# A decoder layer's first two gate/up units: half of the second unit is moved in among the first

## What is computed

```python
mod = jax.nn.silu(c) @ w_ada[l] + b_ada[l]
sh1, sc1, g1, sh2, sc2, g2, sh3, sc3, g3 = jnp.split(mod, 9, axis=-1)
h = modulate(rms_norm(x, norm_ffn1[l]), sh1, sc1)        # h * (1 + scale) + shift
x = x + 0.5 * g1[:, None, :] * swiglu(h, w1_gate[l], w1_up[l], w1_down[l])
```

## Time and profile before

| | before |
|---|---|
| median of three runs | 2169.45 us |
| the profiled execution, its time / its span | 2164.42 / 2162.6 us |
| TensorE matmul, weight load | 96%, 76% busy |
| VectorE, ScalarE, GpSimd | 62%, 42%, 2% busy |
| moved by DMA | 513.21 MB, mean 237 GB/s |
| mean granted TensorE clock | 0.976 |

### The profile page before, as it was taken

One profiled execution on the slowest core, in us unless ns is written; L12 is line 12 of the kernel. 1 busy time (PEld: TensorE's weight loads), 2 busy tenths in 40 slices (PEclk: granted clock), 3 DMA queues, 4 the chain that ended last, 5 costly groups with the idle time before them and its releaser, 6 DMA issues.

```text
span 2162.6 us, 28599 instructions
## 1 busy us (share of the span) xinstructions
PE 2077.0 (96%) x9500; PEld 1633.5 (76%) x9500; DVE 1337.4 (62%) x1774; ACT 904.7 (42%) x1139; POOL 42.8 (2%) x63
## 2 busy tenths in 40 slices
PE   6899999999999999899979899899999999999997
PEld 2468888888877778788847877788888888877776
DVE  1447767677778887866645765577664444444444
ACT  3334444434443333444334544444444444433332
POOL 0100000000000000000004000000000000000000
PEclk7999999999999999999979999999999999999999
DMA  9968787788788888678686405478775666646553
GB/s 363 386 230 288 269 298 272 262 278 286 270 285 311 299 299 303 226 260 287 222 266 226 139 21 179 137 242 275 267 255 182 186 184 184 184 156 222 185 185 127
DMA packets 271077, 513.21 MB, mean 237 GB/s; under 512 B 15193, under 2 KB 29572, under 8 KB 270504
## 3 DMA queue, kind: packets, MB, share of 16 engines
q1 hardware_dynamic: 270120, 508.37, 70.2%
q10 hardware_dynamic: 896, 4.06, 0.5%
HBM read 508.50 MB, written 3.87 MB: 237 GB/s over the span
## 4 chain that ended last, share of the span: by engine, by line
PE 90%; DMA 4%; DVE 3%; issue 1%; ACT 1%; POOL 0%; SPq 0%; DVEq 0%; ACTq 0%; POOLq 0%
PE ps L623 28%; PE ps L624 28%; PE ps L625 28%; DMA ada_half<-in_w_ada_dram 3%; DMA ada_raw<-in_w_cmp_k_dram 1%; PE ps L665 1%; PE ps L707 1%; PE ps L652 1%; PE ps L777 1%; PE ps L681 1%; DMA ada_raw<-in_w_cmp_v_dram 0%; PE ps L733 0%; DVE ada_acc L1450 0%; PE ps L879 0%; PE ps L1039 0%
## 5 line engine op out<-in xcount | busy, mean ns | idle before, releaser
L1432 DVE TENSOR_TENSOR w_lo<-raw,w_hi 128x1024 fp32r<-128x1024 f32 (+1 forms) x657 | 792.5, 1219 | 407.3 <-ACT w_hi L1129 403.3
L1129 ACT ACTIVATE w_hi<-raw 128x1024 fp32r<-128x1024 f32 (+1 forms) x657 | 686.5, 1054 | 815.2 <-PE ps L625 583.9
L623 PE MATMUL ps<-w_hi,hT_hi 128*128 128x512 f32 (+1 forms) x1856 | 741.8, 400 | 8.1 <-POOL hT_lo L584 2.6
L624 PE MATMUL ps<-w_lo,hT_hi 128*128 128x512 f32 (+1 forms) x1856 | 734.2, 396 | 0.0
L625 PE MATMUL ps<-w_hi,hT_lo 128*128 128x512 f32 (+1 forms) x1856 | 733.9, 395 | 0.0
L623 PEld LDWEIGHTS ps<-w_hi,hT_hi 128*128 128x128 f32 x1856 | 351.5, 189 | 96.3 <-issue 7.2
L625 PEld LDWEIGHTS ps<-w_hi,hT_lo 128*128 128x128 f32 x1856 | 351.2, 189 | 84.2
L624 PEld LDWEIGHTS ps<-w_lo,hT_hi 128*128 128x128 f32 x1856 | 351.7, 189 | 82.1 <-issue 1.0
L1450 DVE SCALAR_TENSOR_TENSOR ada_acc<-ada_raw,silu_c,ada_acc 128x512 f32<-128x512 f32 x420 | 315.3, 751 | 7.9
L623 PE MATMUL ps<-w_hi,actT_hi 128*128 128x512 f32 x704 | 283.7, 403 | 3.4 <-DVE silu_gate L1563 3.4
L625 PE MATMUL ps<-w_hi,actT_lo 128*128 128x512 f32 x704 | 279.1, 396 | 0.0
(11 more groups left out here) (202 smaller groups left out, 977.7 us busy)
## 6 DMA issues: line engine op xcount, KB each, us to landing
ada_raw<-in_w_ada_dram SPq DMA_DIRECT2D x224, 512.0 KB, 4.9
raw<-in_w_gate_dram SPq DMA_DIRECT2D x176, 512.0 KB, 4.2
raw<-in_w_up_dram SPq DMA_DIRECT2D x176, 512.0 KB, 4.7
raw<-in_w_down_dram SPq DMA_DIRECT2D x176, 512.0 KB, 4.6
raw<-in_w_in_dram SPq DMA_DIRECT2D x72, 512.0 KB, 4.7
ada_half<-in_w_ada_dram SPq DMA_DIRECT2D x16, 2048.0 KB, 16.3
raw<-in_w_out_dram SPq DMA_DIRECT2D x32, 512.0 KB, 4.4
raw<-in_w_uq_dram SPq DMA_DIRECT2D x9, 512.0 KB, 5.8
```

Of the source, the lines that this page charges most:

```text
L623: pe.matmul(bank, lhs_hi, rhs_hi, start=start, stop=False)
L624: pe.matmul(bank, lhs_hi, rhs_lo, start=False, stop=False)
L1129: act.activation(part(U, w_hi, s), part(U, raw, s), ACT.Copy).then_inc(hi_done, 1)
L1432: dve.tensor_tensor(part(U, w_lo, s), part(U, raw, s), part(U, w_hi, s).bitcast(F32), ALU.subtract)\
```

## The change

The gate panels of the second unit, (1,0), (1,2), ..., (1,14), are taken into the quarters: two of them, (1,4i) and (1,4i+2), follow the first unit's four panels. They accumulate in banks 6 and 7. The eight up panels come behind the last quarter, and the second unit's chunk of the modulation and the first unit's last steps are spread over these. The order of loading follows that (QUARTERS, UP_AFTER), and the raw ring now simply counts on. Because banks 6 and 7 are taken, all start chunks share one row bank (5), which also takes the turned chunks, so a chunk's first half waits until the chunk before has been summed. An even chunk is now a scale and an odd one a shift: the scaling of x starts after the even one, and ScalarE waits for the shift. In TensorE's order halves and panels alternate.

```diff
+QUARTERS = [[(0, 4 * i), (0, 4 * i + 1), (0, 4 * i + 2), (0, 4 * i + 3), (1, 4 * i), (1, 4 * i + 2)] for i in range(4)]
+UP_AFTER = [(1, j) for j in range(1, KD, 2)]
+FIRST_PANELS = [p for quarter in QUARTERS for p in quarter] + UP_AFTER
...
+        order = [(u, j) for u in range(units) for j in range(panels)]
+        if stage == "gu0":
+            order = FIRST_PANELS + order[2 * panels:]
+        for u, j in order:
+            s = n % RING if stage == "gu0" else slot_of(stage, j, last)
...
-    return q % 2 * (START_CHUNKS // 2) + q // 2 if q < START_CHUNKS else q
+    return (1 - q % 2) * (START_CHUNKS // 2) + q // 2 if q < START_CHUNKS else q
...
-        ROW_BANK = (MISC_BANK, T_BANK + 1)
+        ROW_BANK = T_BANK + 1
+        GATE1_BANK = 6
...
@@ SyncE @@
             for q in range(START_CHUNKS // 2):
                 for i in range(4 * q, 4 * q + 4):
                     load_half(i)
-                for j in range(4 * q, 4 * q + 4):
-                    gate_up(0)(Unit("gu0", 0), j)
-            for U in units(sp, "gu0", 1, STAGES["gu0"][0]):
+                for u, j in QUARTERS[q]:
+                    gate_up(0)(Unit("gu0", u), j)
+            for p in range(RING):
+                load_ada(Unit("gu0", 1), 0, p)
+            for i, (u, j) in enumerate(UP_AFTER):
+                gate_up(0)(Unit("gu0", u), j)
+                if RING + i < 8:
+                    load_ada(Unit("gu0", 1), 0, RING + i)
+            for U in units(sp, "gu0", 2, STAGES["gu0"][0]):
                 load_unit(U, gate_up(0))
...
@@ TensorE, start_half @@
-                if i % 2 == 0 and q >= 2:
-                    pe.wait_ge(acc_step, START_STEPS * (q - 1))
+                if i % 2 == 0 and q >= 1:
+                    pe.wait_ge(mod_done, q)
...
+            def second_panel(j):
+
+                panel(Unit("gu0", 1), j, (hT_hi, hT_lo), j // 2 * 2, 2 if j % 2 else GATE1_BANK, j < 2, j >= KD - 2)
...
+            turn_start(0)
             start_half(2)
-            turn_start(0)
-            start_half(3)
             pe.wait_ge(ones_set, 1)
             pe.wait_ge(rev_done, HEADS + 1)
             spread_rstd("ffn1", T_BANK)
             pe.wait_ge(rstd_b_done, 1)
+            turn_norm("ffn1", 0, x_tile)
+            start_half(3)
             for i in range(START_CHUNKS // 2):
                 more = 4 * i + 4 < HALVES
-                turn_norm("ffn1", 2 * i, x_tile)
                 turn_start(2 * i + 1)
+                turn_norm("ffn1", 2 * i + 1, x_tile)
+                first_panel(4 * i)
                 if more:
                     start_half(4 * i + 4)
-                turn_norm("ffn1", 2 * i + 1, x_tile)
+                first_panel(4 * i + 1)
                 if more:
                     start_half(4 * i + 5)
-                first_panel(4 * i)
-                first_panel(4 * i + 1)
+                first_panel(4 * i + 2)
+                if more:
+                    turn_start(2 * i + 2)
+                    turn_norm("ffn1", 2 * i + 2, x_tile)
+                first_panel(4 * i + 3)
                 if more:
                     start_half(4 * i + 6)
-                    turn_start(2 * i + 2)
-                first_panel(4 * i + 2)
-                first_panel(4 * i + 3)
+                second_panel(4 * i)
+                second_panel(4 * i + 2)
                 if more:
                     start_half(4 * i + 7)
+            pe.wait_ge(gu[0]["prod_done"], 2)
+            for _, j in UP_AFTER:
+                second_panel(j)
+                if j == 1:
+                    turn_products(0, Unit("gu0", 0))
+            turn_ada(Unit("gu0", 1), 0)
...
@@ ScalarE, round_hi and the start @@
+                    act.wait_ge(mod_done, r // 2 * 2 + 2)
...
+                hi(Unit("gu0", 1), j)
+                hi(Unit("gu0", 1), j + 2)
+            silu(0, Unit("gu0", 0))
+            for _, j in UP_AFTER:
+                hi(Unit("gu0", 1), j)
+                if j == 3:
+                    actT(0, Unit("gu0", 0))
...
@@ VectorE @@
-                dve.wait_ge(mod_done, 2 * i + 2)
+                dve.wait_ge(mod_done, 2 * i + 1)
...
             add_start(0)
-            add_start(1)
             sum_start(0)
             norm_x("ffn1")
+            first_features(0)
+            add_start(1)
             for i in range(START_CHUNKS // 2):
                 sum_start(2 * i + 1)
-                first_features(i)
                 first_lo(4 * i)
                 round_tmp("ffn1", 2 * i + 1)
                 first_lo(4 * i + 1, 4 * i + 2, 4 * i + 3)
                 if i + 1 < START_CHUNKS // 2:
                     add_start(2 * i + 2)
                     sum_start(2 * i + 2)
+                    first_features(i + 1)
+                second_lo(4 * i, 4 * i + 2)
+                if i + 1 < START_CHUNKS // 2:
                     add_start(2 * i + 3)
+            add_ada(Unit("gu0", 1), 0, 0)
+            product(0, Unit("gu0", 0))
+            for i, (_, j) in enumerate(UP_AFTER):
+                second_lo(j)
+                if i == 1:
+                    actT_low(0, Unit("gu0", 0))
+                if i < 7:
+                    add_ada(Unit("gu0", 1), 0, i + 1)
```

More of the change, by code:

```diff
@@ L85, in count_panels @@
     for stage, (units, panels) in STAGES.items():
[L86 to L92, removed]
+        order = [(u, j) for u in range(units) for j in range(panels)]
[3 more added lines that the diff above has]
+            s = n % RING if stage == "gu0" else slot_of(stage, j, last)
+            uses[s] += 1
+            table[stage, u, j] = (n, uses[s], last[s], s)
+            last[s] = n
+            n += 1
     return table
 def ada_column(q):
-    return q % 2 * (START_CHUNKS // 2) + q // 2 if q < START_CHUNKS else q
+    return (1 - q % 2) * (START_CHUNKS // 2) + q // 2 if q < START_CHUNKS else q
 def count_chunks():
@@ L405, in wait_products, with ada_bank @@
                 eng.wait_ge(mm_done, U.done(STAGES[U.stage][1] - 1))
+        def ada_bank(U):
+            return ROW_BANK if U.stage == "start" or (U.stage, U.first) == ("gu0", 1) else ADA_BANK
         def ada_steps(U, e, n):
@@ L651, in turn_ada @@
                 for b in range(4):
-                    mm = pe.transpose(ps[:, ADA_BANK, b * P:(b + 1) * P], acc[:, a, b * P:(b + 1) * P], ident[:, :])
+                    mm = pe.transpose(ps[:, ada_bank(U), b * P:(b + 1) * P], acc[:, a, b * P:(b + 1) * P], ident[:, :])
                 mm.then_inc(acc_turned, 1)
@@ L664, in start_half @@
                     k, g = i % 2 * HALF + kk, kk % 4
-                    mm = pe.matmul(ps[32 * g:32 * g + 32, ROW_BANK[q % 2], :], silu_pad[:, k, :],
+                    mm = pe.matmul(ps[32 * g:32 * g + 32, ROW_BANK, :], silu_pad[:, k, :],
                                    ada_half[:, i % RING, kk * CW:(kk + 1) * CW], start=k < 4, stop=k >= KD - 4)
@@ L812, in first_rounds @@
                         spread_rstd(n, MISC_BANK)
-            for U in units(pe, "gu0", 1, FF // CW):
+            for U in units(pe, "gu0", 2, FF // CW):
                 gate_up_unit(0, U, False)
@@ L1133, in silu @@
                 act.wait_ge(mm_done, U.done(KD - 2))
+                bank = GATE1_BANK if (U.stage, U.first) == ("gu0", 1) else 0
                 for t in range(TT):
-                    act.activation(act_sg[:, t, :], ps[:, t, :], ACT.Silu).then_inc(gu[f]["silu_done"], 1)
+                    act.activation(act_sg[:, t, :], ps[:, bank + t, :], ACT.Silu).then_inc(gu[f]["silu_done"], 1)
             def actT(f, U):
@@ L1276, in _ @@
                 hi(Unit("gu0", 0), j + 3)
-            for U in units(act, "gu0", 1, 4):
-                gate_up_unit(0, U)
+                hi(Unit("gu0", 1), j)
[5 more added lines that the diff above has]
+                    actT(0, Unit("gu0", 0))
+            gate_up_unit(0, Unit("gu0", 2))
+            gate_up_unit(0, Unit("gu0", 3))
             act.wait_ge(rev_done, HEADS + 1)
@@ L1460, in add_start @@
                     dve.wait_ge(acc_turned, ADA_BEFORE[q][1] + 1)
-                dve.tensor_tensor(acc[:, a, :], ps[:, ROW_BANK[a], :], b_row[:, a, :], ALU.add)\
+                dve.tensor_tensor(acc[:, a, :], ps[:, ROW_BANK, :], b_row[:, a, :], ALU.add)\
                    .then_inc(acc_step, START_STEPS)
@@ L1469, in sum_ada @@
                 dve.tensor_reduce(mod_cols[:, bass.ds(col * 4, 4)],
-                                  ps[:, ADA_BANK, :].rearrange("p (b n) -> p b n", b=4), AX.X, ALU.add)\
+                                  ps[:, ada_bank(U), :].rearrange("p (b n) -> p b n", b=4), AX.X, ALU.add)\
                    .then_inc(mod_done, 1)
@@ L1602, in first_lo, with second_lo @@
                     lo(Unit("gu0", 0), j)
+            def second_lo(*panels):
+                for j in panels:
+                    lo(Unit("gu0", 1), j)
             add_start(0)
-            add_start(1)
             sum_start(0)
             norm_x("ffn1")
+            first_features(0)
+            add_start(1)
```

(6 more changed lines are left out.)

## The result

The changed kernel takes 2202.4 us (median of four runs, 2200.9 to 2205.8) against 2168.7 us; the ratio is 1.0161, 95% interval 1.0141 to 1.0181. It is 33.7 us slower; 28.7 was forecast.

The account below looks back on a forecast made before the run. It took the start as load-bound to 117 us and the rest, from 130 us, as TensorE-bound. Third unit at 218.3 against 189.6, +28.7 us, turned the profiled 2164.4 into 2193.1; forecast 2195.4 us, range 2176 to 2214.

Parts of the forecast that it names:

- The hold on SyncE (a): SyncE's queue: next quarter's halves stand behind gate panels waiting for raw slots, so the stream becomes a loop; DMA idle 13 us.
- gaps of 20 us and more before halves 4, 8 and 12: Sign expected in the changed kernel's SyncE queue, with lo_done as what the halves wait for.
- The first quarter (b): Start, from bias matmuls to first gate/up panel: that panel begins at 50.8 us, 3.1 us earlier than before.
- S0: Start of the first gate/up panel on TensorE, forecast at 50.8 us.
- The loop (c): One quarter's round of landing, TensorE's work, sum and split: 39.8 us, three turns, last quarter's panels 40.7 us later.
- together: Rival in the quarters: the four halves complete together, 55.9 us a turn, +77 us, 2244; chance 0.05.
- cold quarters: Rival on TensorE: clock stays low through panels 4i and 4i+1 of each quarter, 2203 to 2210 us; chance 0.12.
- without that charge the loop would be 38.7: Quarter's loop without the low-clock charge for the half TensorE takes up after its stop.
- The rest (d): From the last quarter's first panel to the third unit: 48.1 us against 60.1, a gain of 12.0, stalls included.
- The sum: All parts together: third unit begins at 218.3 us against 189.6, +28.7 us.
- streams stay full: Rival: SyncE's waits don't hold the halves, a quarter costs its bytes, 30.0 us; -0.7 us, 2166; chance 0.05.
- -6 at most: Most the change could give, with full streams and no stalls between the up panels: -6 us.

Follow-up runs that it names:

- e1: Changed kernel with SyncE sending the next quarter's four halves ahead of the second unit's two gate panels: 2178.1 us, ratio to before 1.0043.
- e2: Kernel before with one added SyncE wait: each later quarter's halves wait until the quarter's first panel is split; 2202.8 us, ratio 1.0156.
- the repeat: Changed kernel, unaltered, run once more for its trace: 2206.1 us (one run).
- e3: Changed kernel with TensorE doing the quarter's last half, its turn and the next norm turn ahead of the two gate panels: 2183.4 us, ratio 1.0066.
- e6: Changed kernel with e3's edit, and SyncE sending three next-quarter halves, the two gate panels, then the fourth half: 2164.0 us, ratio to before 0.9995.
- e7: As e5, with SyncE also sending the first half of a later group ahead of the first unit's third and fourth panels: 2155.1 us, ratio 0.9956.
- e8: As e7, with each later chunk's bias row loaded with its second half instead of its first: 2155.2 us, ratio to before 0.9951.
- e5: As e6, with the first unit's rounding of the turned product and SyncE's ada pairs 4 to 7 one up panel later: 2158.9 us, ratio 0.9962.

## Why the prediction was right, point by point
- **The hold on SyncE (a)** was right in kind and place, and e1 and e2 show it by taking it out and putting it in. The DMA engines are idle from 36 us until (1,0) goes out, at 45.67 in the profile and at 50.84 in the repeat, some 10 and 15 us where I forecast 13. One sign wasn't met: I said gaps of 20 us and more before halves 4, 8 and 12. The longest wait is 18.7 us, and in the later quarters the queue stands in two parts, 7 us for panel (0,4i+2) and 11.7 or 11.4 us for (1,4i), with panels sent between.
- **The first quarter (b).** S0 forecast 50.8, measured 47.57 and 52.75. The term that failed is the bias matmuls, taken at 11.9 us as in before; they are 8.6 or 11.9. With 11.9 the rest was 2 us short: spread, first turn and half 3 also ran at the low clock (half 3 starts at 44.31 in the repeat).
- **The loop (c).** 39.8 forecast, 40.8 measured, three times. From the end of VectorE's split of (0,1), at 48.6 us (row below), the first half is taken up after 9.4, not 9.0; half and panel at the low clock take 6.9, not 6.5; TensorE's 16.2, VectorE's sum at 4.2 and the split at 4.1 are as forecast. The halves landed in order: "together" is out. The half behind the stop ran at the low clock (3.64 us against 1.92), the panel behind it took 3.3 us against 2.8. Panel 4i itself is at the low clock too (47.57 to some 52 us), but that lies under the wait for the half. So "cold quarters" is out as well, though the 2202.4 us measured are its 2203: the time alone wouldn't have told them apart. My "without that charge the loop would be 38.7" is a slip, as 39.8 less 1.6 is 38.2; nothing else used it.

```profile
47.15 1.45 DVE L1473 TENSOR_TENSOR w_lo<-raw,w_hi 128x1024 fp32r<-128x1024 f32 x1 [0.73 <-ACT w_hi L1161]
```

- **The rest (d).** 48.1 forecast, 48.9 measured (170.09 to 219.0). Stops of 1.7 and 3.3 were forecast, 1.34 and 3.46 found, and one of 0.41 that wasn't foreseen: the next up panel's load too comes just late. I had put no low clock behind these stops, and in both traces of this kernel there was none. Had it come as in e3 and e6, where the two turns of products lie 34.3 us apart instead of 32.6, the part would have been near 51.
- **The sum.** Third unit forecast at 218.3, found at 219.0 in a profile with the quick start. That they lie so close is luck: S0 came 3.2 us early and the loops and the rest took 3.9 too long. In the repeat, with S0 at 52.75, it is 224.1. Against before's profile 219.0 is 29.4 us later; the execution's time, though, is 39.3 us longer, of which 8.6 lie in the attention stretch and about 1 between. I said that nothing behind the third unit changes; for the instructions that holds, for the granted clock it didn't. Between medians it is 33.7. Of the 5 us that my 28.7 is short, the loops' 3 x 1.0 and the tail's 0.8 are accounted for. The other 1 can't be assigned: start and attention differ by more than that from one execution to the next. The bounds that I gave for the parts add up to 2178 to 2208; the range of 2176 to 2214 goes by the rivals.
- **The rival "streams stay full"** was priced wrongly, and with it the bound "-6 at most". I let each quarter cost its bytes, 30 us, counted from S0. But the stream starts at 3 us, far ahead of S0; with a full stream the end is set by all the bytes up to the last half. In e7 the last quarter's chunk is turned at 125.5 us, and the third unit begins at 172.8, 16.8 us ahead of before in the profiles and 9.5 us by the medians (2155.1 against 2164.6). The profile flatters it by the quick start, and 5.1 us are lost again in the attention stretch; in e8, whose bias matmuls take 11.9 us as before's do, the third unit is 12.6 us ahead. So the idea of the change had a gain in it that the rival's sum hid.

## What to carry to other kernels
A queue that issues in program order carries every wait for a buffer to all that stands behind it: when transfers are moved, ask of each one what it waits for, and put behind it only what isn't needed sooner than that wait ends. Once a load waits for a use that waits for the load before, the time of a round is the whole chain, landing time, the consumer's backlog and the hand-overs, and no longer the bytes. For the bound of a stream that is never dry, count its bytes from its own start, not from the first use.

## What the runs showed of the hardware
The granted clock in a stretch of short matmuls isn't the same in all executions: the bias matmuls of one program took 8.6 or 11.9 us, and the attention stretch 191 us at 1.00 or 196 to 200 us at a mean of 0.87 to 0.94 over its first 80 us (e5 and e7 have 0.94). Either shifts a single profile by 3 to 9 us in a place that the change doesn't touch; the runs of the kernel before spread over 11 us (2161.7 to 2172.4).
